# The factor chains of the second softmax, written with plain operands

## The reference, cut to what matters

```
s = jnp.where(mask, q.k * scale + bias, -inf)
p = softmax(s)                       # two of them, n = 0 and 1
a = p[:, :, 0] - lam * p[:, :, 1]
o = rmsnorm(a @ v, g_sub) * (1 - lam_init)
```

## Time and profile before

| what | value |
|---|---|
| median of 3 runs | 2805.71 us (2801.96 to 2806.47) |
| the profiled execution | 2801.12 us |
| its span | 2799.4 us |
| PE busy | 2725.3 us, 97% |
| DVE busy | 1756.6 us, 63% |
| ACT busy | 1344.5 us, 48% |
| POOL busy | 629.6 us, 22% |

### The profile page before, as it was taken

One profiled execution on the slowest core, in us unless ns is written; L12 is line 12 of the kernel. 1 busy time (PEld: TensorE's weight loads), 2 busy tenths in 40 slices (PEclk: granted clock), 3 DMA queues, 4 the chain that ended last, 5 costly groups with the idle time before them and its releaser, 6 DMA issues.

```text
span 2799.4 us, 36795 instructions
## 1 busy us (share of the span) xinstructions
PE 2725.3 (97%) x13362; PEld 2253.3 (80%) x13362; DVE 1756.6 (63%) x2495; ACT 1344.5 (48%) x2413; POOL 629.6 (22%) x558
## 2 busy tenths in 40 slices
PE   8999999989999999999999999999999999999998
PEld 6888888878787787877788788888888888888887
DVE  6211111169889889899846778887777544435567
ACT  5121111168788788788523545464444433322233
POOL 5220021026746646556411100000000000000012
PEclk9999999999999999999999999999999999999999
DMA  5443343464434514414346755565345555546566
GB/s 190 131 153 101 104 136 113 144 148 98 105 83 97 128 52 118 123 41 120 106 128 217 260 204 199 186 237 201 134 149 196 180 186 209 185 159 224 203 219 240
DMA packets 287660, 434.49 MB, mean 155 GB/s; under 512 B 19648, under 2 KB 134592, under 8 KB 287488
## 3 DMA queue, kind: packets, MB, share of 16 engines
q1 hardware_dynamic: 241664, 368.41, 42.4%
q10 hardware_dynamic: 45056, 63.05, 6.2%
q0 software_dynamic: 768, 0.79, 0.1%
HBM read 280.27 MB, written 151.91 MB: 154 GB/s over the span
## 4 chain that ended last, share of the span: by engine, by line
PE 68%; DVE 5%; ACT 4%; issue 3%; POOL 0%; ACTq 0%; POOLq 0%; DVEq 0%
PE ml_ps L2845 7%; PE ml_ps L2843 7%; PE ml_ps L2844 7%; PE ml_ps L2813 7%; PE ml_ps L2815 7%; PE ml_ps L2816 7%; PE at_ps_t L1486 5%; PE at_ps_s L1462 4%; PE at_ps_s L1468 3%; PE mo_acc L1801 2%; PE mo_acc L1803 2%; PE mo_acc L1802 2%; PE at_ps_o L1501 2%; PE at_ps_o L1502 2%; ACT at_probs L1313 2%
## 5 line engine op out<-in xcount | busy, mean ns | idle before, releaser
L1361 DVE TENSOR_REDUCE at_nmax<-at_ps_s 128x1 f32<-128x1024 f32 (+7 forms) x384 | 346.6, 906 | 37.0 <-PE at_ps_s L1468 34.8
L2813 PE MATMUL ml_ps<-ml_h_hiM,ml_w_hi 128*128 128x512 f32 x896 | 349.1, 390 | 1.0 <-DVE ml_t L2635 0.9
L2816 PE MATMUL ml_ps<-ml_h_hiM,ml_w_lo 128*128 128x512 f32 x896 | 348.7, 389 | 0.0
L2815 PE MATMUL ml_ps<-ml_h_loM,ml_w_hi 128*128 128x512 f32 x896 | 348.7, 389 | 0.0
L2845 PE MATMUL ml_ps<-ml_b_hi,ml_a_lo 128*128 128x512 f32 x896 | 348.6, 389 | 0.0
L2844 PE MATMUL ml_ps<-ml_b_lo,ml_a_hi 128*128 128x512 f32 x896 | 348.6, 389 | 0.0
L2843 PE MATMUL ml_ps<-ml_b_hi,ml_a_hi 128*128 128x512 f32 x896 | 348.6, 389 | 0.0
L598 DVE SCALAR_TENSOR_TENSOR pj_out_sb<-pj_acc,pj_out_sb 128x512 fp32r<-128x512 f32 x96 | 66.4, 691 | 424.1 <-ACT pj_out_sb L534 424.1
L1370 DVE TENSOR_TENSOR at_p_lo<-at_ps_t,at_p_hi 128x512 fp32r<-128x512 f32 x480 | 280.0, 604 | 35.8 <-ACT at_p_hi L1331 32.7
L1331 ACT ACTIVATE at_p_hi<-at_ps_t 128x512 fp32r<-128x512 f32 x480 | 248.5, 533 | 87.6 <-PE at_ps_t L1486 48.0
L2490 POOL TENSOR_SCALAR ml_ss<-ml_ss 128x1 f32<-128x1 f32 x16 | 17.6, 1099 | 1183.7 <-ACT ml_junk L2583 1183.4
(11 more groups left out here) (264 smaller groups left out, 5981.3 us busy)
## 6 DMA issues: line engine op xcount, KB each, us to landing
ml_a_raw<-ua SPq DMA_DIRECT2D x112, 512.0 KB, 3.9
qk<-pj_out_sb ACTq DMA_DIRECT2D x64, 512.0 KB, 2.8
ml_w_raw<-in_w_up_dram SPq DMA_DIRECT2D x64, 512.0 KB, 5.1
ua<-ml_t SPq DMA_DIRECT2D x128, 256.0 KB, 2.6
ml_b_raw<-in_w_down_dram SPq DMA_DIRECT2D x56, 512.0 KB, 4.9
at_q<-qk SPq DMA_DIRECT2D x96, 256.0 KB
at_k<-qk SPq DMA_DIRECT2D x96, 256.0 KB
ua<-ml_x SPq DMA_DIRECT2D x96, 256.0 KB, 2.6
```

What stands on the lines that cost most here:

```text
L1361: dve.tensor_reduce(nmax[:, par, sc.a, s, sc.part:sc.part + 1], ps_s[:, sc.g % 2, 0:sc.width], AX.X, ALU.max, negate=True).then_inc(maxed, 1)
L2813: pe.matmul(to, hi, h_hi[m][:, k, :], start=begins and k == 0, stop=False, skip_group_check=not begins)
L2815: pe.matmul(to, hi, h_lo[m][:, k, :], start=False, stop=False, skip_group_check=not begins)
L2816: last = pe.matmul(to, lo, h_hi[m][:, k, :], start=False, stop=k == 3, skip_group_check=not begins)
```

## The change

The chain with two parts takes both corrected row sums in one product and one sum over two columns, in place of two instructions of one column each. Three instructions that took a column as a per-row scalar take it as a plain operand. The sum now waits for the product. The planner's hold of a `chain` goes to 0.85 us with two parts and to 0.44 us with one, and with that the order that it writes may differ anywhere in attention. The number of instructions stays five and two.

```diff
-                walk.step("chain", (b.n, sc.a), "DVE", 1.12 if two else 0.5, at + RUSH["chain"],
+                walk.step("chain", (b.n, sc.a), "DVE", 0.85 if two else 0.44, at + RUSH["chain"],
...
                         sums = total[:, par, a, :]
-                        link(dve.tensor_scalar(sums[:, 0:1], rsum[:, par, a, 0, 0:1], corr[:, par, a, 0:1],
-                                               rsum[:, par, a, 0, 1:2], ALU.mult, ALU.add), False)
-                        link(dve.tensor_scalar(sums[:, 1:2], rsum[:, par, a, 1, 0:1], corr[:, par, a, 1:2],
-                                               rsum[:, par, a, 1, 1:2], ALU.mult, ALU.add))
+                        link(dve.tensor_tensor(sums, rsum[:, par, a, :, 0], corr[:, par, a, :], ALU.mult))
+                        link(dve.tensor_tensor(sums, sums, rsum[:, par, a, :, 1], ALU.add))
                     link(dve.reciprocal(factor[:, par, a, 1:2], sums[:, 1:2]))
-                    link(dve.tensor_scalar(factor[:, par, a, 0:1], sums[:, 0:1], nlam[:, :], factor[:, par, a, 1:2],
-                                           ALU.mult, ALU.mult), last.parts == 2)
+                    link(dve.scalar_tensor_tensor(out=factor[:, par, a, 0:1], in0=sums[:, 0:1], scalar=nlam[:, :],
+                                                  in1=factor[:, par, a, 1:2], op0=ALU.mult, op1=ALU.mult),
+                         last.parts == 2)
                     if last.parts == 2:
-                        link(dve.tensor_scalar(factor[:, par, a, 1:2], factor[:, par, a, 0:1], corr[:, par, a, 1:2],
-                                               None, ALU.mult), False)
+                        link(dve.tensor_tensor(factor[:, par, a, 1:2], factor[:, par, a, 0:1], corr[:, par, a, 1:2],
+                                               ALU.mult), False)
```

## The result

The changed kernel took 2838.76 us (median, 2837.4 to 2842.14) against 2805.85: a ratio of 1.0124, interval 1.011 to 1.0138. It is 1.2% slower; the forecast was 0.1% faster, with a range of 2794 to 2812 us. The profiled execution took 2837.4 us, its span 2835.6. The last value product of attention starts at 1374.0 us before and 1410.3 us after, so all 36 us are lost in attention.

What follows compares the result with a forecast made beforehand. PE was taken to bound attention (busy 94%), its rests being all a faster DVE could give back. The median 2805.7 us, less 3.2 us from shorter chains, with reordering at zero, gave 2802.5 us; range 2794 to 2812.

Steps and rivals of the forecast that it cites:

- The bound and the length of a chain: Attention: PE bounds the stage; a two-part chain on DVE falls from 1.11 to 0.88 us, one-part from 0.38 to 0.32.
- two bounds: Saving on the path in attention: at least 1.8 us (eight chains on it), at most 4.6 us (where DVE leads).
- The list of waits: What PE rests for in attention: `exp` freeing score slots 41.3 us, `lo` freeing transpose slots 16.0, `mix` on DVE 6.2.
- The bounds of the new forms: New DVE chain instructions priced by neighbours: product and sum 150 ns, at most 266; factor 214 ns, between 154 and 274.
- the ends of DVE's time: Range for DVE's time in all chains, from +5.8 us with dear new forms to -13.1 us with a cheap factor.
- The path: Of 9.3 us less DVE time in attention's chains, 3.2 us shortens the path; PE's cover hides the others.
- The order at zero: Reordering of attention by the planner's new holds costed at zero in the middle, with ends of 10.4 us either way.
- The rival on this side: Slower through the order: a `mix` taken before a `max` on DVE, 1.3 us each, 2812.9 us at eight places; chance 0.22.

Runs made afterwards that it cites:

- order-only run: Kernel before with its old instructions, but the planner's new holds (0.85 and 0.44): 2821.89 us, ratio 1.0067.
- two harmless orders: Kernel before, old instructions, only the planner's holds changed: 1.04 and 0.53 gave 2806.39 us (1.0011); 1.03 and 0.48 gave 2809.1 us (1.0016).
- four losing orders: Kernel before, old instructions, other planner's holds: 0.85/0.44 (2821.89 us), 0.85/0.50 (2853.64 us), 1.12/0.44 (2822.6 us), 1.12/0.38 (2830.94 us).
- 0.85 with 0.50: Kernel before, old instructions, only the planner's two-part hold new (0.85, one part kept at 0.50): 2853.64 us, ratio 1.0182.

## Why the prediction was wrong

**The bound and the length of a chain: right where GpSimd is idle.** A chain of two parts takes 0.90 us against 0.88, one of one part 0.32 as forecast; the product, the sum and the factor take 151, 161 and 220 ns against 150, 150 and 214; and with GpSimd nearly idle 3.8 us are gained against 3.2. That 3.8 and 3.2 lie so close is partly luck: 3.2 was the middle of two bounds, for a kernel with GpSimd at work. The list of waits skipped one of 8.4 us in 11 waits (PE for L1414 on DVE), which no term uses.

**The bounds of the new forms: wrong.** This is the first step that failed. It said that a product costs 150 ns and at most the 266 it replaces, and took the ends of DVE's time as +5.8 and -13.1 us. The product's mean was 486 ns and its longest 1642; by summed durations the chains went from 51.4 to 64.7 us, 13 more where 13 less were expected. The instructions alone cost 0.69%. The neighbours for the price were chosen by shape and count of scalars, not by where their inputs lie. The trace of before had the row. The mix of 640 columns, two inputs from SBUF, is longer than that of 1024:

```profile
L1404 DVE SCALAR_TENSOR_TENSOR at_probs<-at_probs,at_factor 128x640 f32<-128x640 f32 x4 | 6.0, 1510 | 0.0
```

It starts at 695.05 us beside GpSimd's L1222 and ends 0.68 us after it. GpSimd's next add is then the one that is held, 2.95 us for 1024 columns where others take 2.40:

```profile
693.52 2.37 POOL L1222 TENSOR_TENSOR at_probs<-at_probs 128x1024 f32<-128x1024 f32 x1 [4.94 <-ACT at_probs L1320]
695.84 2.95 POOL L1226 TENSOR_TENSOR at_probs<-at_probs 128x1024 f32<-128x1024 f32 x1
```

In the changed kernel the same mix comes before both adds and takes 0.88 us. The Trainium skill (SBUF — State Buffer, "SBUF: two separate sides") says it outright: VectorE, with two SBUF inputs, and a GpSimd instruction that reads SBUF take one pair of ports in turn, as an exclusive lock for the whole instruction. I had looked up the cost of the operations there and not of their operands. The traces agree, but for one thing: GpSimd's power of four columns (L1285, 1.02 us) held nothing. In the changed kernel a sum of 0.16 us and a factor of 0.22 us run inside it in each of the four heads.

**The path: right in kind, blind to the clock.** That PE's rests are all there is to gain or to lose assumed a full clock. Half of the loss, 18 us, is PE working at the lower level around and after rests of 4.2 us. The forecast had no term for it.

**The order at zero: wrong.** This is the second step that failed. It compared each hold with the trace (1.12 with 1.11, 0.85 with 0.88) and took a true hold for a good order. The new order costs 17 to 20 us alone, where even the end of that term was 10.4. The truest holds of all for the old instructions (1.12 and 0.38) give 2831 us. The planner is greedy: a shorter step lets another one go first, and its own end shows it.

The rival on this side, with a chance of 0.22, named half of the cause, the order. Its mechanism is there too: in the planner's new list for VectorE two mixes of each head stand ahead of reductions that they stood behind, three and one, eight mixes in the four heads as the rival had it. In the order-only run one such place is

```profile
756.69 1.00 DVE L1399 SCALAR_TENSOR_TENSOR at_probs<-at_probs,at_factor 128x128 f32<-128x128 f32 x1
757.62 1.27 DVE L1404 SCALAR_TENSOR_TENSOR at_probs<-at_probs,at_factor 128x1024 f32<-128x1024 f32 x1
758.82 0.55 DVE L1361 TENSOR_REDUCE at_nmax<-at_ps_s 128x1 f32<-128x384 f32 x1
```

where before the reduction came at 753.62 us and the mixes behind it. That this is what costs the time isn't shown: the two harmless orders have the same move at this place. What they don't have, and all four losing orders do, is the mix of the block with `J` = 1 ahead of reductions of the next block, one to four of them; no run moves it alone. At the place above PE rests for two reasons, scores that come late because value products were taken ahead of them, and the mix behind them:

```profile
756.47 0.45 PE L1462 MATMUL at_ps_s<-at_k,at_q 128*128 128x384 f32 x1 [1.42 <-ACT at_probs L1313]
...
758.95 1.91 PE L1486 MATMUL at_ps_t<-at_ident_r,at_probs 128*128 128x128 f32 x9 [1.75 <-DVE at_probs L1404]
```

**Open:** which displaced step starts the loss of the order, whether the planner's own end or the distance from the old order foretells it, and how much of the extra loss of 0.85 with 0.50, which its own end doesn't show, comes from the longer mixes of VectorE.

## What to carry to other kernels

Before an instruction on VectorE gets a second SBUF operand, look at what GpSimd does beside it: a per-row scalar costs some 60 ns more and can save up to 2 us. Price an instruction by a row with its operands in the same memories and the same neighbour running. Where a planner writes the order, compare its own end before and after: a cost that is lowered can lengthen the plan, as 784.0 to 793.4 us here, and that can be read before anything runs. Here a longer plan went with a slower kernel in all four cases.

## What the runs showed of the hardware

A VectorE instruction of one column with two tensor inputs in SBUF took up to 2.42 us beside GpSimd's 1024-column add (2.41 us), and 0.15 without. A tensor_scalar on the same columns (196 to 207 ns), a reciprocal (0.14 to 0.17 us) and the `lo` with one input in PSUM (0.67 to 0.69 us for 512 columns) didn't change beside the same work. It goes the other way too: GpSimd's add took 2.95 us in place of 2.40 where a held VectorE instruction of 640 columns went first. In the changed kernel the grant fell around the end of a rest of PE of 4.2 us, four times, and stayed at the lower level for 7 to 10 us; in the order-only run it was there for 3 to 7 us in each head, though no rest was longer than 2.5 us.
